# Eight expert-weight slots in rotation, a re-timed set of cache copies and contiguous weight layouts in a one-core decoder step

## The reference

```
h = RMSNorm(x); z = h @ w_in                       # 1024 -> 8704: LRU x, LRU gate, q, k, v, two merge gates
A = RG-LRU(conv4(z_x)) * gelu(z_gate) @ w_br_lru
B = dilated attention over 3 groups of 4 heads @ w_br_att    # samples: keys and values from the caches
x += (sigmoid(g_a) * A + sigmoid(g_b) * B) @ w_out
x += MoE(RMSNorm(x))                               # 32 experts, top 4, 1024 -> 2*1024 -> 1024
x += sigmoid(RMSNorm(x) @ w_ple_gate) * (p @ w_ple)
```

## Time and profile before

| | us |
|---|---|
| median of 3 runs | 1416.43 (1415.73 to 1416.78) |
| the profiled execution, its own time | 1418.05 |
| span of the profiled execution (first to last instruction) | 1416.4 |
| PE busy in the span | 1350.0 (95%) |
| first product of expert 0 | 442.33 |
| mean TensorE clock granted | 0.989 of full |

### The profile page before, as it was taken

How to read it: one execution, slowest core, us unless ns; L and a number is a source line. 1 busy time by engine, 2 the same in 40 slices (tenths; PEclk the granted TensorE clock), 3 DMA queues, 4 the chain that set the end, 5 groups by cost and what they waited for, 6 DMA issues and landing times.

```text
span 1416.4 us, 17044 instructions
## 1 busy us (share of the span) xinstructions
PE 1350.0 (95%) x7000; PEld 676.8 (48%) x7000; DVE 399.8 (28%) x636; ACT 182.4 (13%) x340; POOL 35.6 (3%) x62
## 2 busy tenths in 40 slices
PE   7999599899999999999999999999999999999988
PEld 6887488798874333333333333333333333333337
DVE  4106547320233222222222122221222212222134
ACT  1111034322003100010001000010000100000101
POOL 0001003000000000000000000000000000000000
PEclk9999899999999999999999999999999999999999
DMA  9889997958986999999999999999999999999980
GB/s 385 312 345 326 304 353 259 294 137 328 376 308 242 400 422 429 428 428 428 428 428 428 428 428 428 427 429 427 428 428 427 430 427 429 426 429 428 428 344 31
DMA packets 44886, 531.41 MB, mean 375 GB/s; under 512 B 6973, under 2 KB 7373, under 8 KB 16533
## 3 DMA queue, kind: packets, MB, share of 16 engines
q1 hardware_dynamic: 40784, 471.47, 80.9%
q10 hardware_dynamic: 1685, 54.43, 10.6%
q0 software_dynamic: 2384, 5.03, 1.2%
HBM read 526.15 MB, written 58.38 MB: 413 GB/s over the span
## 4 chain that ended last, share of the span: by engine, by line
PE 59%; DMA 39%; ACT 1%; DVE 0%; issue 0%; SPq 0%; DVEq 0%
DMA ring<-in_wmoe 33%; PE PS L789 25%; PE PS L522 16%; DMA ring<-in_win 5%; PE PS L829 2%; PE PS L726 2%; PE PS L691 2%; PE PS L803 2%; DMA ring<-in_w_ple_gate 2%; PE PS L937 1%; PE PS L947 1%; PE PS L701 1%; PE PS L568 1%; PE PS L815 1%; PE PS L795 1%; ACT Zb L1124 1%
## 5 line engine op out<-in xcount | busy, mean ns | idle before, releaser
L789 PE MATMUL PS<-ring,Zb 128*64 128x512 f32 x3072 | 687.6, 596 | 20.2 <-DMA ring<-in_wmoe 19.2
L789 PEld LDWEIGHTS PS<-ring,Zb 128*64 128x64 f32 x3072 | 209.4, 137 | 421.7 <-issue 378.7
L522 PE MATMUL PS<-hT,ring 128*128 128x264 f32 x1024 | 237.9, 392 | 21.8 <-DMA ring<-in_win 21.8
L522 PEld LDWEIGHTS PS<-hT,ring 128*128 128x128 f32 x1024 | 195.4, 193 | 58.5 <-DMA ring<-in_win 22.4
L1451 DVE TENSOR_TENSOR xc<-xc,PS 128x528 f32<-128x528 f32 x128 | 89.7, 701 | 171.8 <-PE PS L829 159.5
L1479 DVE COPY Zb<-PS 128x512 f32<-128x512 f32 x32 | 22.1, 692 | 326.7 <-PE PS L789 326.7
L829 PE MATMUL PS<-Zb 64*128 64x264 f32 x496 | 88.7, 435 | 0.0
L829 PEld LDWEIGHTS PS<-Zb 64*128 64x128 f32 x496 | 37.3, 184 | 100.6 <-issue 100.6
L1132 ACT ACTIVATE Zb<-Zb 128x512 f32<-128x512 f32 x32 | 20.2, 630 | 470.2 <-DVE Zb L1461 470.2
L1124 ACT ACTIVATE Zb<-PS 128x512 f32<-128x512 f32 x32 | 19.1, 597 | 358.0 <-PE PS L817 358.0
L803 PE MATMUL PS<-Zb 128*64 128x512 f32 x256 | 63.5, 617 | 0.0
(11 more groups left out here) (246 smaller groups left out, 844.6 us busy)
## 6 DMA issues: line engine op xcount, KB each, us to landing
ring<-in_wmoe SPq DMA_DIRECT2D x192, 2048.0 KB, 22.8
ring<-in_win SPq DMA_DIRECT2D x16, 2048.0 KB, 15.5
out_kvs<-in_cache ACTq DMA_DIRECT2D x8, 4032.0 KB, 28.9
out_kvs<-in_cache ACTq DMA_DIRECT2D x8, 1984.0 KB, 13.2
ring<-in_kt SPq DMA_DIRECT2D x2, 2048.0 KB, 24.5
ring<-in_cache SPq DMA_DIRECT2D x2, 2048.0 KB, 10.8
ring<-in_w_br_lru SPq DMA_DIRECT2D x2, 2048.0 KB, 17.9
ring<-in_w_out SPq DMA_DIRECT2D x2, 2048.0 KB, 19.6
```

Of the source, the lines that this page charges most:

```text
L522: last = mm(PS[:, bank, 0:T], w[:, k, :], (lt if piece == 0 else hT)[:, k, :], start=(k == 0), stop=(k == KT - 1))
L789: last = mm(PS[CAP * h:CAP * (h + 1), bank, :], src[:, k, f:f + CAP], w[:, k, h * CH:(h + 1) * CH], start=(slot == 4 and k == 0), stop=(sl ...
```

## The change

- Two more slots for expert weights. `hT` and `lt` become two parts of one tensor `hl`, and its first 4096 columns are slot 6; the tiles of `w_ple`, `pT`, `w_router` and `rparts` share one tensor `zone` of 4096 columns, which is slot 7. The 6 x 32 pieces go through the eight slots in rotation (`place`), and the pattern repeats every four experts. Pieces 0 and 1 of expert 1 are loaded into slots 6 and 7 before the loop; every later piece waits for the use of the piece eight before it.
- SP's and PE's expert loops cover four experts per pass. PE's first four and last four experts stand outside. ACT, DVE and POOL keep their loops.
- The g = 2 cache copies are issued behind tiles 15, 25, 38, 42 and 53 and when `bl_mm`, `ba_mm` reach 2 and `wo_mm` reaches 1.
- `w_router`, `w_ple`, `w_br_lru`, `w_br_att`, `w_out`, `w_ple_gate` and the strided cache values come in layouts in which each partition reads one run; the values of g = 2 come in one load instead of two.
- `b_down` is loaded behind `satt` (sample attention added) and signals `wpl_in`; one DVE semaphore becomes a link; `w_ple_gate` waits for the end of expert 30 instead of the gate product of expert 31.

```
+        hl = sb("hl", [P, 2 * KT * T])
+        hT = hl[:, 0:KT * T].rearrange("p (k t) -> p k t", t=T)
+        lt = hl[:, KT * T:2 * KT * T].rearrange("p (k t) -> p k t", t=T)
...
+        slots = [ring[:, s, :] for s in SLOT] + [hl[:, 0:4096], zone]
+        def place(j, s):
+            return (6 * j + s) % 8, (6 * j + s) // 8
...
-            sp.wait_ge(S.at_pv, 8)
-            cached_v(2)
-            cached_v(2, 64)
+            sp.wait_ge(S.at_pv, 8)
+            cached_v(2)
...
-                sp.dma_start(view, w[k0 * P:(k0 + 4) * P, :].rearrange("(k p) n -> p k n", p=P)).then_inc(sem, 16)
+                sp.dma_start(view, w[k0 // 4]).then_inc(sem, 16)
...
-            sp.dma_start(bdn, a["b_down"]).then_inc(S.bdn_in, 16)
+            sp.wait_ge(S.satt, 1)
+            sp.dma_start(bdn, a["b_down"]).then_inc(S.wpl_in, 16)
...
+            sp.wait_ge(S.ss_sum, 2)
+            sp.dma_start(slots[6], weights(1, 0)).then_inc(S.w6, 16)
+            sp.wait_ge(S.pl_mm, KT)
+            sp.dma_start(slots[7], weights(1, 1)).then_inc(S.w7, 16)
+
+            def load(e, j, n, pieces=range(6)):
+                for s in pieces:
+                    if s < 2:
+                        sp.wait_ge(used[s + 4], n - 1)
+                    else:
+                        sp.wait_ge(used[s - 2], n)
+                    at = place(j, s)[0]
+                    sp.dma_start(slots[at], weights(e, s)).then_inc(full[at], 16)
+
+            load(1, 1, 1, range(2, 6))
+            load(2, 2, 2)
+            load(3, 3, 3)
...
+            with sp.Fori(1, E // 4) as i:
+                for j in range(4):
+                    load(4 * i + j, j, 4 * i + j)
...
-            sp.wait_ge(S.g1_mm, E)
+            sp.wait_ge(S.d1_mm, E - 1)
             half(a["w_ple_gate"], 0, wpg[0], S.wpg_in)
...
+            def half_product(bank, src, slot, i, j):
+                at, fill = place(j, slot)
+                pe.wait_ge(full[at], 16 * (3 * i + fill + 1))
+                w = slots[at].rearrange("p (k n) -> p k n", k=4)
...
-            with pe.Fori(2, E - 1) as e:
-                block_(e)
-            block_(E - 1, following=False)
+            for j in range(4):
+                block_(0, j)
+            with pe.Fori(1, E // 4 - 1) as i:
+                for j in range(4):
+                    block_(i, j)
+            for j in range(4):
+                block_(E // 4 - 1, j, following=(j < 3))
...
-            with act.Fori(1, 6) as i:
+            with act.Fori(1, 4) as i:
                 for t in range(4):
                     evac(4 * i + t, t)
                 shift(0, i)
                 shift(1, i)
-            for b in range(3):
-                shift(2, b)
+            shift(2, 0)
+            with act.Fori(4, 6) as i:
+                for t in range(4):
+                    evac(4 * i + t, t)
+                shift(0, i)
+                shift(1, i)
...
-                if n in (35, 43, 51):
-                    shift(2, n // 8 - 1)
+                if n in (25, 38, 42, 53):
+                    shift(2, (25, 38, 42, 53).index(n) + 1)
...
+            act.wait_ge(S.bl_mm, 2)
+            shift(2, 5)
+            act.wait_ge(S.ba_mm, 2)
+            shift(2, 6)
             act.wait_ge(S.wo_mm, 1)
-            for b in range(6, NS):
-                shift(2, b)
+            shift(2, 7)
...
-            TT(X, X, xc[:, :, :], ALU.mult).then_inc(S.lru_x, 1)
+            link(TT(X, X, xc[:, :, :], ALU.mult))
```

More of the change, by code:

```diff
@@ L204, in __init__ @@
         self.w5 = sem("w5")
+        self.w6 = sem("w6")
+        self.w7 = sem("w7")
         self.g0_mm = sem("g0_mm")
@@ L336, in build @@
         sgp = Z[:, 0:KT, :]
-        wpg = [ring[:, SLOT[s], :].rearrange("p (k n) -> p k n", k=4) for s in (0, 1)]
+        slots = [ring[:, s, :] for s in SLOT] + [hl[:, 0:4096], zone]
+        wpg = [slots[s].rearrange("p (k n) -> p k n", k=4) for s in (0, 1)]
+        def place(j, s):
+            return (6 * j + s) % 8, (6 * j + s) // 8
         def load_most(eng):
@@ L342, in load_most, with further @@
             return eng.value_load(most, min_val=0, max_val=T)
-        def further(eng, count, block_of, first, last, before=None, after=None):
+        def further(eng, count, block_of, first, last, before=None, after=None, fours=False):
             def chunk(c):
@@ L349, in chunk @@
                     before(c)
-                with eng.Fori(0, E) as e:
-                    block_of(e, e + c * E)
+                if fours:
+                    with eng.Fori(0, E // 4) as i:
+                        for j in range(4):
+                            block_of(i, j, i + c * (E // 4))
+                else:
+                    with eng.Fori(0, E) as e:
+                        block_of(e, e + c * E)
                 if after is not None:
@@ L455, in weights @@
+            sp.dma_start(bdn, a["b_down"]).then_inc(S.wpl_in, 16)
             def weights(e, s):
                 return a["wmoe"][e][s]
-            def slot(s):
-                return ring[:, SLOT[s], :]
-            full = (S.w0, S.w1, S.w2, S.w3, S.w4, S.w5)
+            full = (S.w0, S.w1, S.w2, S.w3, S.w4, S.w5, S.w6, S.w7)
             used = (S.g0_mm, S.g1_mm, S.u0_mm, S.u1_mm, S.d0_mm, S.d1_mm)
-            sp.dma_start(slot(0), weights(0, 0)).then_inc(S.w0, 16)
+            sp.dma_start(slots[0], weights(0, 0)).then_inc(S.w0, 16)
@@ L465, in _ @@
             sp.wait_ge(S.bl_mm, KT)
-            sp.dma_start(slot(1), weights(0, 1)).then_inc(S.w1, 16)
-            sp.dma_start(slot(2), weights(0, 2)).then_inc(S.w2, 16)
+            sp.dma_start(slots[1], weights(0, 1)).then_inc(S.w1, 16)
+            sp.dma_start(slots[2], weights(0, 2)).then_inc(S.w2, 16)
             sp.wait_ge(S.ba_mm, KT)
-            sp.dma_start(slot(3), weights(0, 3)).then_inc(S.w3, 16)
+            sp.dma_start(slots[3], weights(0, 3)).then_inc(S.w3, 16)
             sp.wait_ge(S.wo_mm, KT)
-            sp.dma_start(slot(4), weights(0, 4)).then_inc(S.w4, 16)
@@ L472, in _ @@
[L472 to L480, removed]
-            count = load_most(sp)
[L482 to L485, removed]
@@ L487, in _ @@
-            sp.wait_ge(S.g1_mm, E)
+            sp.dma_start(slots[4], weights(0, 4)).then_inc(S.w4, 16)
+            sp.dma_start(slots[5], weights(0, 5)).then_inc(S.w5, 16)
+            sp.wait_ge(S.ss_sum, 2)
[6 more added lines that the diff above has]
+                        sp.wait_ge(used[s + 4], n - 1)
+                    else:
+                        sp.wait_ge(used[s - 2], n)
+                    at = place(j, s)[0]
+                    sp.dma_start(slots[at], weights(e, s)).then_inc(full[at], 16)
@@ new lines, in _ @@
+            load(1, 1, 1, range(2, 6))
+            load(2, 2, 2)
+            load(3, 3, 3)
+            count = load_most(sp)
+            with sp.Fori(1, E // 4) as i:
+                for j in range(4):
+                    load(4 * i + j, j, 4 * i + j)
+            further(sp, count, lambda i, j, m: load(4 * i + j, j, 4 * m + j), first=lambda: sp.wait_ge(S.d1_mm, E),
+                    last=lambda: sp.wait_ge(S.yb_zero, 1), after=lambda n: sp.wait_ge(S.d1_mm, n), fours=True)
+            sp.wait_ge(S.d1_mm, E - 1)
@@ L743, in _ @@
             last.then_inc(S.ss_sum, 1)
-            pe.wait_ge(S.wpl_in, 32)
+            pe.wait_ge(S.wpl_in, 48)
             def ple(m):
@@ L839, in spread_bias, with block_ @@
                 last.then_inc(S.c_mm, 1)
-            def block_(n, following=True, alone=False):
+            def block_(i, jn, following=True, alone=False):
+                n = 4 * i + jn
                 def between(j):
@@ L902, in _, with apart @@
             pe.wait_ge(S.gT_ok, 1)
-            pe.wait_ge(S.bdn_in, 16)
-            block_(0)
-            block_(1)
+            for j in range(4):
+                block_(0, j)
             count = load_most(pe)
-            with pe.Fori(2, E - 1) as e:
-                block_(e)
-            block_(E - 1, following=False)
-            def apart(e, n):
+            with pe.Fori(1, E // 4 - 1) as i:
+                for j in range(4):
+                    block_(i, j)
+            for j in range(4):
+                block_(E // 4 - 1, j, following=(j < 3))
+            def apart(i, j, m):
+                n = 4 * m + j
                 rows(n)
                 rows_T(n)
-                block_(n, following=False, alone=True)
+                block_(m, j, following=False, alone=True)
                 spread_all(n)
             further(pe, count, apart, first=lambda: spread_all(E - 1), last=lambda: pe.wait_ge(S.yb_zero, 1),
-                    after=lambda n: pe.wait_ge(S.added, 4 * n + 4))
+                    after=lambda n: pe.wait_ge(S.added, 4 * n + 4), fours=True)
             pe.wait_ge(S.added, 4 * E)
@@ L1634, in cols, with rows_in, halves @@
         return np.ascontiguousarray(v.transpose(1, 0, 2))
+    def rows_in(w):
+        return np.ascontiguousarray(w.reshape(-1, P, w.shape[1]).transpose(1, 0, 2))
```

(10 more changed lines are left out.)

48 lines of the change are left out of this document (18 added, 30 removed).

## The result

The changed kernel takes 1405.6 us in the median of 4 runs (1403.85 to 1406.08), against 1416.08 (1414.91 to 1416.78) for the kernel before. The ratio on record is 0.9911, with an interval of 0.9891 to 0.9931; the two medians as they stand give 0.9926. That is 10.5 us saved where 34.3 were forecast. It lies outside the range of 1375 to 1401, and on the rival to which I gave 0.04, "moves the copies, not the stalls" (1406).

What follows compares the result with a forecast made beforehand. Bounds: PE's two waits for `w_in` pieces (26.4 us), then full DMA engines in the expert stage (about 22 us lost). Gains 16.3 + 8.1 + 9.9 = 34.3 us against 1418.05 give 1383.8, as a median 1382; range 1375 to 1401.

Steps and rivals of the forecast that it cites:

- moves the copies, not the stalls: Rival: other `w_in` pieces (11, 12, 15) wait as long and only the two slots' gain remains; 1406, chance 0.04.
- Part 1, first stall: PE's wait for `w_in` piece 10 before tile 40: moved copies cut 18.3 us to 2, gain 16.3.
- the bookkeeping at 147 us: Bytes queued when piece 10 is issued: 18.0 MB demand less 15.9 moved leaves 2.1 MB; piece 10 lands at 159.6.
- the many small stores behind tile 31: Rival before tile 40: they slow everything near 140 us, 8 to 14 us of stall stay; 1388 to 1394, chance 0.15.
- Part 1, second stall: PE's wait for `w_in` piece 14 before tile 56: nothing remains, as no copy starts with it; gain 8.1 us.
- Part 2: Expert stage: two more slots put two pieces on their way before PE's first product; gain 9.9 us, bounds 0 to 9.9.
- no lead: Rival at the expert stage: late copies eat the room, slots 6 and 7 land too late; 1392, chance 0.08.
- Part 3: The rest: contiguous layouts, moved waits and loop of four gain zero; the DVE link is below 0.1 us.
- The loop of four: Expert loop; rival that its instructions are fetched again every pass: 1400 (chance 0.07) or 1421, slower (chance 0.04).

Runs made afterwards that it cites:

- e12: The changed kernel with only the router bias load moved from behind piece 7 of `w_in` to the start; 1398.87 us, 0.9886.
- e6: The changed kernel with POOL gathering its short convolution and state rows so that each partition stores one run; 1394.1 us, 0.984.
- e1: The changed kernel with the cache copies issued where the kernel before had them; 1404.56 us, 0.9922.
- e10: The kernel before with only the contiguous layouts of the weights and cache values; 1416.26 us, ratio 1.0.
- e9: The changed kernel with the large copy behind tile 25 issued behind tile 61 instead; 1382.15 us, 0.977.
- e11: The changed kernel with large copies at the start and behind tiles 7, 40, 42 and 61, and three late; 1402.99 us, 0.9894.

## Why the prediction was wrong, and where it was right

**Part 1, first stall: wrong.** Forecast +16.3, measured -7.9. The step that failed is the bookkeeping at 147 us: "2.1 MB are left ... 2.1 MB and piece 10 take 4.2 / 0.332 = 12.7 us". It counted bytes over both queues, as if piece 10 had only its share of a common pool ahead of it. Piece 10 landed at 185.8 instead of 159.6, 40.6 us after its issue. Three things stand against the step.

First, the loads of SP's queue land in their order, and the copies take most of the engines' time: their packets are larger (41 KB in the mean above, a weight piece has rows of 16 KB) and go one for one, so 69 to 97 us moved 8.98 MB in q10 and 1.75 in q1 (4.98 and 4.21 before). I had such a split in the earlier trace rows and used only its sum. The list of what was still to come at 97 us had 1.3 MB of the copy behind tile 15 and no piece 8; in the run the copy was through by then, and piece 8, 2.1 MB, had not begun. What was left at 147 was above all the gate weights, which stand ahead of piece 10; they landed at 174.9. With 1.0 MB of copies and 0.9 of POOL's it was 4.0 MB, not 2.1. That alone, with piece 10, would be 6.1 / 0.332 = 18.4 us, a landing near 165; the larger part of the miss is not in that count.

Second, the bias: 6.5 us of the stall, shown by e12. I had no term for it: before, no large copy was under way when it was issued.

Third, the rate: I took the 332 GB/s of the earlier trace rows, and the stretch 132 to 165 moved 180. Up to 155 POOL's short stores stand in it (134 to 155: 182 GB/s), then POOL's two rotary DMAs with no copy beside them (155 to 165: 164 GB/s); e6 shows 332 over the whole with the short stores made long, and 4.88 MB of SP's queue instead of 2.42. The text named "the many small stores behind tile 31" for a rival, with 8 to 14 us, and didn't price them in the forecast. And as piece 10 hadn't landed by 160.19, the copy behind tile 38, which I had ruled out beside it, went out beside it after all: 147 to 186 moved 5.1 MB in q10, 4.1 of them this copy, and 5.2 in q1.

How large each cause is depends on the others: without the bias 6.5 us of the 26.2 go, with long stores 13.4 (10.06 + 9.91 - 7.12 = 12.9 are left), with one copy fewer all but a trace. With the same short stores the stretch 132 to 165 moves 258 GB/s before, 249 in e12 and 180 here. Most of that is the copies that happen to lie in it (before, e12 and the changed kernel in turn):

```profile
q10 hardware_dynamic: 136, 5.81, 55.7%
q1 hardware_dynamic: 139, 2.02, 30.7%
...
q1 hardware_dynamic: 208, 3.10, 46.1%
q10 hardware_dynamic: 122, 4.16, 36.0%
...
q1 hardware_dynamic: 165, 2.42, 47.6%
q10 hardware_dynamic: 97, 2.55, 32.9%
```

So 180 is not a rate that the short stores set by themselves, and SP's queue got no less there than before.

**Part 1, second stall: right,** forecast 8.1, measured 7.8. **Part 2: right in mechanism and near in size.** Forecast 9.9; 11.4 by the profiles of the two kernels (12.6 of span less 1.2 ahead of the experts), and 10.4 by that of e1 (span 1402.9, first product 439.24: 13.5 less 3.1). The room that I had found for it, the 3 GB/s of 434 to 446, is what it filled. Both are a little above the bound of 9.9; where the rest comes from was not looked into. The late copies didn't eat it; "no lead" falls. **Part 3: right for the layouts,** zero by e10; the moved waits and the DVE link were not run alone.

**The loop of four: not fetched again.** The instruction queue q8 within the first pass (560 to 657 us), and below it all queues of 660 to 1240 us, where the next passes run:

```profile
q8 instruction: 4, 0.07, 0.3%
...
q1 hardware_dynamic: 17027, 248.00, 100.5%
q0 software_dynamic: 640, 0.17, 0.1%
```

No q8. The loop of 1148 PE records, 4.4 blocks, comes once and stays. The Trainium skill, "Runtime: NRT & Kernel Launch", section "Instruction fetch mechanics", has a window of two pages, by which it would be fetched again, and a larger memory for PE, in which it would stay; this trace speaks for the second.

**The rivals.** The one that came true has the right size for a wrong reason: its waits were to be at pieces 11, 12 and 15, and were at 9 and 10. What it said of part 2, that it alone remains, is what e1 shows. The forecast of 1382 was that of a kernel in which tile 40 doesn't wait: e9 is that kernel, with 1382.15 us and the first product at 415.28 (forecast near 418). The miss lies in the one wait. That the two times agree to 0.2 us is luck: the runs of e9 lie between 1379.74 and 1387.44, and it has one of the copies elsewhere.

## What to carry to other kernels

Bytes are not the measure of what stands ahead of a transfer: go through its own queue in order, and count packets, since two busy queues share by packets. A small table in many short rows, ahead of urgent weights, costs one large packet of the other queue for each of its packets on an engine; load such tables where nothing large is under way. When a change moves background copies, ask of each stretch what the queue with the deadline still has to send by then, and take its rate from its own bytes in a stretch with the same short stores and copies in it, not from the sum of the queues.

## What the runs showed of the hardware that I had not expected

The 128 rows of a table of 16 KB held their queue for 15.4 us beside another queue's large copies, 1.4 without them, and those of a table of 1 KB for 20.9 (e11; 2.7 in the changed kernel). Short stores of 0.1 MB in all went with 180 to 258 GB/s at a DMA share of about 1 (three kernels), where the same bytes in long runs leave 332 (e6). And 33 MB of copies in the background cost about 4 us in the whole kernel when they are placed as in e9 (1382.15 against 1378.55 without them), and 27 when they are placed as in the change.
